# Expert weight loads whose partitions take neighbouring rows, with strided transposes to match

## What is computed

```python
def hier_moe(h, w_rg, b_rg, w_re, b_re, w_gate, w_up, w_down):   # h: (T, 1024)
    ...
    # each token goes to 2 of 32 experts; its rows are gathered into blocks of one expert each
    xb = h[slot_tok].reshape(n_blocks, DISPATCH_BLOCK, D)

    def expert_block(args):
        xe, e = args
        hid = jax.nn.silu(xe @ w_gate[e]) * (xe @ w_up[e])
        return hid @ w_down[e]
    ...
```

## Time and profile before

| | before |
|---|---|
| median of 3 runs | 1268.18 us |
| the profiled execution | 1268.83 us |
| its span, first to last instruction | 1267.1 us |
| mean granted clock of TensorE | 0.932 of full speed |
| PE busy | 1103.5 us, 87% of the span |
| DVE, ACT, POOL busy | 42%, 39%, 19% |
| DMA | 303.45 MB, a mean of 239 GB/s |
| loads of w_exp_gate and w_exp_up | 256 of 512 KB |
| loads of w_exp_down | 64 of 1024 KB, median 12.8 us from issue to landing |

### The profile page before, as it was taken

How to read it: one execution, slowest core, us unless ns; L and a number is a source line. 1 busy time by engine, 2 the same in 40 slices (tenths; PEclk the granted TensorE clock), 3 DMA queues, 4 the chain that set the end, 5 groups by cost and what they waited for, 6 DMA issues and landing times. The chain is left out here.

```text
span 1267.1 us, 17601 instructions
## 1 busy us (share of the span) xinstructions
PE 1103.5 (87%) x5202; PEld 628.9 (50%) x5203; DVE 530.9 (42%) x712; ACT 492.9 (39%) x669; POOL 237.3 (19%) x267
## 2 busy tenths in 40 slices
PE   3799995598589968899999999897999797967997
PEld 3699984487478744233333333232333232326885
DVE  4468986677622237211121122222123222136886
ACT  4333444334322124433244355444355454343332
POOL 1024572443500000110111011000101011002320
PEclk9899996799788969899999999898999899998999
DMA  6041913211111494996688999999999999945651
GB/s 208 27 116 37 286 23 138 101 50 50 51 50 55 153 347 190 368 360 210 238 300 312 367 351 398 396 398 396 397 395 397 398 397 394 403 157 195 220 187 63
DMA packets 150176, 303.45 MB, mean 239 GB/s; under 512 B 12144, under 2 KB 42896, under 8 KB 150139
## 3 DMA queue, kind: packets, MB, share of 16 engines
q1 hardware_dynamic: 135787, 267.83, 57.6%
q0 software_dynamic: 6512, 22.29, 5.1%
q10 hardware_dynamic: 7840, 12.85, 2.8%
HBM read 262.77 MB, written 40.16 MB: 239 GB/s over the span
## 5 line engine op out<-in xcount | busy, mean ns | idle before, releaser
L1682 PE MATMUL ps_gate_up<-weights,x_turned 128*64 128x512 f32 x1568 | 362.0, 616 | 9.5 <-issue 8.8
L104 ACT COPY weights<-raw_weights 128x2048 f32 (+1 forms) x96 | 180.6, 1899 | 148.7 <-DMA raw_weights<-w_exp_up 64.6
L104 DVE COPY weights<-raw_weights 128x2048 f32 (+1 forms) x96 | 117.6, 1231 | 260.0 <-PE ps_gate_up L1682 107.7
L1682 PEld LDWEIGHTS ps_gate_up<-weights,x_turned 128*64 128x64 f32 x1568 | 112.4, 141 | 225.5 <-issue 224.6
L1695 PE MATMUL ps_y<-weights,h_turned 128*64 128x512 f32 x784 | 180.7, 603 | 3.1 <-ACT h_turned L1614 3.1
L737 DVE SCALAR_TENSOR_TENSOR taps_bank<-a_ext,par,taps_bank 128x640 f32<-128x640 f32 (+1 forms) x152 | 119.7, 787 | 4.0
L1643 DVE TENSOR_TENSOR hidden<-ps_gate_up,act_gate 128x256 f32<-128x256 f32 x49 | 20.8, 425 | 231.2 <-ACT act_gate L1607 231.2
L109 POOL COPY token_ids<-item_tokens 128x1 int32 (+1 forms) x49 | 8.9, 181 | 532.9 <-PE ps_x L1669 496.4
L381 POOL TENSOR_TENSOR conv_pool_taps<-conv_pool_taps,tap_product 128x640 f32<-128x640 f32 (+1 forms) x64 | 91.7, 1433 | 60.4 <-ACT tap_product L468 54.4
L1695 PEld LDWEIGHTS ps_y<-weights,h_turned 128*64 128x64 f32 x784 | 52.4, 137 | 97.1 <-issue 93.7
L468 ACT ACTIVATE tap_product<-a_ext,par 128x640 f32<-128x640 f32 (+1 forms) x80 | 58.1, 745 | 41.3 <-POOL conv_pool_taps L381 27.4
(11 more groups left out here) (255 smaller groups left out, 1566.2 us busy)
## 6 DMA issues: line engine op xcount, KB each, us to landing
raw_weights<-w_exp_gate SPq DMA_DIRECT2D x128, 512.0 KB
raw_weights<-w_exp_up SPq DMA_DIRECT2D x128, 512.0 KB
raw_weights<-w_exp_down SPq DMA_DIRECT2D x64, 1024.0 KB, 12.8
y_rows<-y_tile ACTq DMA_DIRECT2D x98, 128.0 KB
y_rows<-zero_rows SPq DMA_DIRECT2D x16, 512.0 KB, 6.2
x_rows<-x_tile SPq DMA_DIRECT2D x9, 512.0 KB, 2.6
h_rows<-h_tile SPq DMA_DIRECT2D x9, 512.0 KB, 2.9
proj_rows<-projected SPq DMA_DIRECT2D x9, 512.0 KB, 2.6
```

The costliest lines, as they stand in the source:

```text
L104: copy(S.work[s][:, :], raw).then_inc(S.w_ready[s], 1)
L1682: last = pe.matmul(ps_gu[side[j], :, :], x_t[:, c, side[of]], w[:, :, share(D_EXP, j)], start=(k == 0), stop=(k == KD - 1))
```

## The change: what it does

Each partition takes rows that are neighbours in memory. Within each half of 512 channels, partition p has rows 4 p to 4 p + 3 of w_gate and w_up; a piece takes two of the four. In a down piece, partition p has rows 2 p and 2 p + 1. So that the channels on the partitions of `x_t` and `h_t` agree with that, the four transposes of x take every fourth column, starting at column 0 to 3, and the two of `hid` every second column. The number of loads, their bytes, their places in SBUF and their order are as before, and so are the matmuls.

```diff
@@ -83,14 +83,14 @@  load_piece
     if s in GU:
-        rows = slice(2 * P * s, 2 * P * s + 2 * P)
+        of, c = divmod(2 * s, KD // SIDES)
         for m in range(2):
-            eng.dma_start(raw.rearrange("p (k m n) -> p k m n", k=2, m=2)[:, :, m, :],
-                          S.w_experts[m][0, e, rows, :].rearrange("o (k p) n -> p (o k) n", p=P)).then_inc(S.raw_loaded[s], 16)
+            w = S.w_experts[m][0, e, of * D // SIDES:(of + 1) * D // SIDES, :].rearrange("o (p c) n -> p (o c) n", p=P)
+            eng.dma_start(raw.rearrange("p (k m n) -> p k m n", k=2, m=2)[:, :, m, :], w[:, c:c + 2, :]).then_inc(S.raw_loaded[s], 16)
     else:
         first = 2 * P * (s - DOWN[0])
         eng.dma_start(raw.rearrange("p (k n) -> p k n", k=2),
-                      S.w_experts[2][0, e, first:first + 2 * P, :].rearrange("o (k p) n -> p (o k) n", p=P))\
+                      S.w_experts[2][0, e, first:first + 2 * P, :].rearrange("o (p k) n -> p (o k) n", p=P))\
            .then_inc(S.raw_loaded[s], 16)
@@ -1666,7 +1666,7 @@  turn_x
-                        last = pe.transpose(ps_x[:, k, :], x[:, k * P:(k + 1) * P], S.ident[:, :])
+                        last = pe.transpose(ps_x[:, k, :], x[:, k::KD // SIDES], S.ident[:, :])
@@ -1699,7 +1699,7 @@  turn_hid
-                        last = pe.transpose(ps_h[:, k, :], hid[:, k * P:(k + 1) * P], S.ident[:, :])
+                        last = pe.transpose(ps_h[:, k, :], hid[:, k::KE // SIDES], S.ident[:, :])
```

## The result

The changed kernel takes 1270.48 us (median of 20 runs, 1267.22 to 1274.49), the kernel before beside it 1267.72 us (20 runs, 1265.25 to 1270.67). In the table, an item's length is the time from one gate_up to the next, and a disturbed item is the prediction's item in trouble: one that waits for its expert's weights.

A forecast was written before the change was run, and what follows sets the result against it. Transfers of expert weights were taken to bound the kernel from 760 to 1086 us; down loads -2.8 us, all other terms 0, so 1268.18 - 2.8 = 1265.4 us, range 1254 to 1277 us.

The forecast's parts named there:

- What bounds the kernel: Expert stage, 760 to 1086 us: transfers of expert weights set the pace; 45.7 us lost, all that faster loads could return.
- Down loads: Loads of w_exp_down: 8 KB runs instead of 4 KB save 0.15 us per expert, 2.8 us in all.
- Gate and up loads: Expert gate and up loads: destination still 2 KB runs, so 0 saved; other end 0.61 us per expert.
- Outside the stretch: Before 760 us and in experts 0 and 1: faster loads cost and give nothing; uncovered, 0.3 us together.
- Transposes: TensorE's weight loads of x and `hid` with a step: taken as 0, bounds 0 to 112 ns per load.
- Rival 3: Strided weight loads in turn_x cost 112 ns each, 0.45 us per item: 8.5 us slower, 1277 us; chance 0.15.
- Rival 1: Gate and up loads behave as 4 KB too: 14.1 us saved, 1254 us, or some 1260; chance 0.27.
- Rival 2: Down loads' 8 KB runs are cut into two of 4: nothing changes in transfers, 1268.2 us; chance 0.10.
- Rival 4: New addresses make gate and up loads 5% slower: 7.2 us more, 1275 us; chance 0.10.
- The sign of being wrong: Prediction is wrong if the stretch at DMA share 1.04 shortens by more than 5 us or lengthens at all.

The follow-up runs named there:

- 4 KB layout: The change, with each gate and up piece laid out by matrix first, so its destination is one 4 KB run too; ratio 0.9966 to the kernel before.

## Why the prediction was right and wrong

**It said 1265.4 us and faster; it is slower, by 2.7 us.** The measured time lies within the range of 1254 to 1277 us, on the side that the forecast gave 0.22. Step by step:

- *What bounds the kernel.* Right: the stretch from 760 to 1086 us and its lost 45.7 us. With the 4 KB layout the 23 items of it take 300.7 us instead of 311.5.
- *Down loads.* Right: 8192 packets fewer, and 17.04 us for a disturbed item where 17.05 was said. Loads alone gave 2.9 us (0.6 to 5.1) for the 2.8 of the sum, the traces 1.9. The fixed 9.5 ns per run, drawn from two rates, foretold the disturbed item; the rates themselves hang on the window by some 2% (before, neighbouring windows of down loads read 403 to 416 GB/s), so that 422 measured for 422 estimated is partly luck.
- *Gate and up loads.* Right to take 0: 387 GB/s again, and no packet fewer. The section of the Trainium skill that I set beside it (DMA: Bandwidth & Descriptors, "Why a DMA increments its semaphore by 16 and not by 1") says that one descriptor moves one contiguous run of the last dimension. The packet count of the change agrees with it; with the 4 KB layout two such rows that touch on both sides went as one packet. Reads widened over rows without the writes do not show as fewer packets or a higher rate in any run.
- *Outside the stretch.* Nothing in these runs speaks against it.
- *Transposes: this is the step that failed.* "I take 0, by the row of the same instruction." The reasoning was that 64 and 128 columns load in 137 and 140 ns, so the reading of columns is hidden. The duration showed the step: 213 ns. A row that varies the number of neighbouring columns says nothing of how a column is read when it has no neighbour. The bound was sound, 0 to 112 ns, and the value is 73 and 64 ns, but the point that decides, 28 ns on four loads, stood near enough to 0 that the term with the widest bounds should have carried the forecast. Of the 73 ns some 22 reach PE's pace; but hidden's two loads pay as well, which neither the rival nor the rule beside it allowed, and the six together cost 0.16 us per item, 4.0 us for 25 items (3.8 us read off 23 of them), more than the loads bring.
- *Rival 3* is thus what happened, in a milder form and on both tiles. The Trainium skill (SBUF — State Buffer, "Door 1: The DMA port swizzle") has lines of 16 bytes that want at least two accesses each. As the prediction read it, fp32 may step by two for free and pays at four. The runs do not show that for this operand: 205 to 209 ns with two, 213 with four, 140 with one.
- *Rivals 1, 2 and 4* are out: packets and the disturbed item stand against the first two, the loads alone against the fourth.
- *The sign of being wrong* looked past the mistake. It asked whether the stretch bound by transfers gets longer, or shorter by more than 5 us. From the 24th gate_up to the 47th it got 1.2 us shorter, while the loss came from the items outside it. The sign that did speak was the other one, an undisturbed item of 11.72 us where 11.56 was said.

By the terms the sum is -2.8 + 4.0 = +1.2 us, just under the interval of 1.5 to 3.8 around the 2.7 that were measured; with 1.9 us for the loads, as the traces have it, it is about +2. Whether anything beyond scatter is left stays open. One thought is that items within the stretch let some of PE's longer pace through. The traces do not show it: with the old loads the stretch took 311.51 us without the steps and 309.82 with all of them, with the new loads 309.55 and 310.26, and both differences lie within its scatter.

## What to carry to other kernels

The length of a transfer's run was the shorter of its two sides' in all three layouts here: look at the destination before paying for a better source. Where a layout for DMA puts a step on an operand of TensorE, price that step on every instruction that reads it and count how many of them lie on the pace of the engine that is busy most of the time; 0.16 us per item outweighed a faster transfer that helps in the second half of the items only. And where the gain forecast is 0.2%, the term that is least known decides the sign, not the one worked out best.

## What the runs showed of the hardware that I had not expected

- A stationary float32 operand with a step of 8 or 16 bytes takes 205 to 213 ns to load instead of 140; of that 0.02 to 0.03 us per load shows in the spacing of the transposes.
- DVE pays for steps too, on either side, but not for all: a product of 256 columns takes 425 ns, 620 when it writes with a step of 512 bytes, and 424 when it reads SBUF and PSUM with a step of 8 bytes and writes in a row. The norm of 1024 columns goes from 1285 ns to 2025 when it writes with a step of 512 bytes and to 2127 when it reads with one of 32 bytes.
- Loads of 2, 4 and 8 KB runs read 387, 410 and 422 GB/s in short windows, which shift by some 2% with the window. An estimate from the first two, 9.5 ns per run and 75.2 ns per 2 KB on each of 16 engines, foretold to 0.1 us by how much a disturbed item gets shorter: from 17.21 to 17.04 us, and with 4 KB runs in gate and up to 16.43 to 16.53 us.
